# Latent attention's gate product dealt out between the rounds of attention, and the last additions in another order

## The chip, the cores and the metric

The kernel runs on one core of a Trainium2 chip. What is measured is the device time of one execution in microseconds. The kernel before takes 1385.15 us (median of three, 1384.3 to 1385.21).

## The reference

Two transformer blocks over 512 tokens of 1024 features, all in float32. The first puts 16 meta tokens ahead of the sequence and mixes in three ways: a short convolution, latent attention with a gate, and retention.

```python
(cx, cb, cc, cz, cq, ckv, krope, mz, rq, rk, rv, rz) = jnp.split(u @ w_in[l], IN_OFFSETS, axis=-1)
y_conv = short_conv_mixer(cx, cb, cc, cz, ...)      # b * conv3(c * x) * silu(z)
y_mla = mla_mixer(cq, ckv, krope, mz, ...)          # 8 heads, chunked mask; softmax(q k) v * silu(mz)
y_ret = retention_mixer(rq, rk, rv, rz, ...)        # 4 heads, rotary q and k; rms_norm(o) * silu(rz)
h = h + jnp.concatenate([y_conv, y_mla, y_ret], axis=-1) @ w_out[l]
```

The second block has gated linear attention, sparse attention, attention to a memory of 256 rows, and a mixture of 16 experts of which each token takes two:

```python
hid = jax.nn.silu(hf @ w_gate[e]) * (hf @ w_up[e])
out = sum over the two chosen experts of share * (hid @ w_down[e])
x + out
```

## The kernel before

All five engines walk through one list of steps that `make_order` writes, and each issues its own instructions of a step. Nothing else sets the order: if a step stands later in the list, it stands later in the queue of every engine that has to do with it. Engines wait for each other by counters; a wait holds up all that is queued behind it on its engine.

A dense product in full precision is made of three matmuls, high part by high part, high by low and low by high (`product`, L1036 to L1038). Weights come in units of two chunks of 128 rows by 512 columns; SyncE loads them, ScalarE writes the high part (L1801), GpSimd the low part (L917), four units ahead at most. A "part" is what one unit adds to one of four PSUM banks: six matmuls of 512 columns. A product by 1024 features has four units and so 16 parts (and, for retention, four short ones for the meta rows, in bank 4).

The stretch in question: the latent part, the queries and keys of latent attention (`w_uq`, `w_ukv`), the two convolution products `conv_a` and `conv_b`, the convolution itself on VectorE (`conv`, L3046 to L3058), the rotation and scaling of queries (VectorE, L3139 to L3143) and keys (GpSimd, L928, L930) in `mla_norm`, the gate product `mla_z`, and then `mla_order`: 16 rounds, m = 0 to 15, four for each pair of heads, in which the query tile is m % 4. A round does two heads, j = 2m and 2m + 1:

- `mla_scores`: a TensorE product (L1202), VectorE's maximum (L3153), ScalarE's exp (L2315)
- `mla_prob`: VectorE divides by the sum (L3163, L3166)
- `mla_turn`: TensorE transposes the probabilities, first the 16 meta columns into bank 4 (L1209), then the others into bank 6 (L1212); VectorE copies the first (L3172), ScalarE the others (L2323)
- `mla_values`: TensorE, for the round before (L1227, L1230); behind the fourth tile VectorE multiplies by the gate (L3179)

The scores of a round with the last tile are 528 wide and take part of bank 4 too, so that they wait until VectorE has copied the meta columns of the head before. Every new pair begins with `mla_transposes` of its two heads (L1181 to L1187), copied by ScalarE (L2301, L2307).

Between these stand the steps that `take` deals out, two parts or one step of retention at a time: the products `ret_qk` and `ret_vz`, retention's transposes, scores, values and turns for each pair of its heads, and one unit of the output product `w_out0`. Then `mix_mla` writes high and low parts of the gated output (L2368, L2519).

`ret_qk` is rotated by VectorE in `rope_turn`: four products of the PSUM bank with cosine or sine into the temporaries t0 to t3 (L2534 to L2537), and from these a difference and a sum (L2539, L2540). There is one set of temporaries.

At the very end stands `last_rows`: experts 14 and 15 are visited last, and their share is added through one-hot products instead of memory. `down` writes a visit's output into banks 5 and 6, ScalarE and VectorE make high and low parts (L2068, L3014), TensorE spreads them to the tokens (L1640, L1641) in eight banks by `ROW_BANKS`. The other experts' rows come back by gathers from GpSimd's queue (L994), two for each token tile; `add(t)` scales and adds them (L3026, L3028), and L3038 adds the one-hot rows; SyncE stores each tile.

## Time and profile before

| | us |
|---|---|
| median of three runs | 1385.15 |
| the profiled execution | 1386.81 |
| its span | 1385.0 |
| TensorE busy | 1294.7 |
| VectorE busy | 644.0 |
| ScalarE busy | 633.8 |
| GpSimd busy | 408.7 |

The rounds of latent attention lie between 139 and 304 us of the span, the last down product begins at 1361.7 us. Times in the rows are from the start of the span. In the timelines a row is one instruction or several like it, and what stands in brackets is how long its engine had been idle and what ended that. The granted clock (PEclk) is 1.00 for TensorE at 2.4 GHz and 0.50 at 1.2 GHz; a mean between says how the stretch is divided. A matmul's end is modelled, so starts are the safer numbers.

### The profile page before, as it was taken

The numbers are of one execution on the slowest core, as the hardware profiler recorded it, in microseconds if no ns is written. First come the engines' busy times: TensorE is split into PE (matmuls) and PEld (weight loads), VectorE is DVE, ScalarE is ACT, GpSimd is POOL, SyncE is SP. The second block draws the span as 40 slices with busy tenths as digits, with TensorE's granted clock in tenths as the row PEclk, the third lists the DMA queues.
The fourth block names the chain that finished last, engine by engine and source line by source line (L and its number), as shares of the span: only waits on it lengthen the run. The fifth ranks groups of instructions, "written<-read, shape, count | busy, mean of one in ns | idle before, by whom it ended". The sixth has DMA issues, their size and how long they took to land.

```text
span 1385.0 us, 16953 instructions
## 1 busy us (share of the span) xinstructions
PE 1294.7 (93%) x6321; PEld 1000.8 (72%) x6321; DVE 644.0 (46%) x1423; ACT 633.8 (46%) x1105; POOL 408.7 (30%) x202
## 2 busy tenths in 40 slices
PE   5999889879989999999998998999999999899996
PEld 4798666557768777775887786888787777676764
DVE  3255354535230125236898444314334133777775
ACT  5443434343552457445334545333433323577771
POOL 4265221014655341232533222444105431100002
PEclk9999999979999999999999999999999999999998
DMA  5243423013445221221332111342107430799935
GB/s 166 66 127 107 136 94 122 18 60 117 152 132 167 77 73 50 61 77 46 112 94 69 47 55 60 114 152 79 36 1 257 180 140 36 296 420 412 421 147 199
DMA packets 76317, 179.13 MB, mean 129 GB/s; under 512 B 11184, under 2 KB 22758, under 8 KB 69574
## 3 DMA queue, kind: packets, MB, share of 16 engines
q1 hardware_dynamic: 68528, 164.96, 34.8%
q0 software_dynamic: 2592, 8.40, 1.6%
q10 hardware_dynamic: 5110, 4.62, 1.2%
q8 instruction: 53, 0.87, 0.3%
q14 instruction: 34, 0.28, 0.1%
HBM read 152.79 MB, written 25.17 MB: 128 GB/s over the span
## 4 chain that ended last, share of the span: by engine, by line
PE 81%; DVE 10%; ACT 4%; issue 3%; DMA 1%; POOL 0%; SPq 0%; DVEq 0%; ACTq 0%; POOLq 0%
PE ps L1036 20%; PE ps L1037 20%; PE ps L1038 20%; PE ps L1574 4%; PE ps L1202 1%; PE ps L1442 1%; PE ps L1425 1%; PE ps L1558 1%; DVE mix_lo L2519 1%; DVE work L2740 1%; PE ps L1398 1%; PE ps L1230 1%; DVE best L2738 1%; PE ps L1470 1%; PE ps L1432 1%
## 5 line engine op out<-in xcount | busy, mean ns | idle before, releaser
L917 POOL TENSOR_TENSOR w_lo<-raw,w_hi 128x1024 fp32r<-128x1024 f32 (+1 forms) x158 | 378.2, 2408 | 754.8 <-ACT w_hi L1801 745.9
L1801 ACT ACTIVATE w_hi<-raw 128x1024 fp32r<-128x1024 f32 (+1 forms) x158 | 159.8, 1032 | 170.4 <-PE ps L1038 162.1
L1036 PE MATMUL ps<-w_hi,act_hi 128*128 128x512 f32 (+1 forms) x560 | 232.3, 415 | 3.1 <-DVE gate L2601 0.9
L1037 PE MATMUL ps<-w_lo,act_hi 128*128 128x512 f32 (+1 forms) x560 | 219.1, 391 | 0.0
L1038 PE MATMUL ps<-w_hi,act_lo 128*128 128x512 f32 (+1 forms) x560 | 218.3, 390 | 0.0
L1036 PE MATMUL ps<-w_hi,mix_hi 128*128 128x512 f32 x320 | 132.8, 415 | 7.7 <-DVE mix_lo L2519 6.4
L1036 PEld LDWEIGHTS ps<-w_hi,act_hi 128*128 128x128 f32 (+1 forms) x560 | 104.3, 186 | 40.3 <-issue 11.9
L1037 PE MATMUL ps<-w_lo,mix_hi 128*128 128x512 f32 x320 | 127.0, 397 | 0.0
L1038 PE MATMUL ps<-w_hi,mix_lo 128*128 128x512 f32 x320 | 126.8, 396 | 0.0
L1038 PEld LDWEIGHTS ps<-w_hi,act_lo 128*128 128x128 f32 (+1 forms) x560 | 104.0, 186 | 24.9
L1037 PEld LDWEIGHTS ps<-w_lo,act_hi 128*128 128x128 f32 (+1 forms) x560 | 104.2, 186 | 23.7 <-issue 1.2
L1036 PE MATMUL ps<-act_hi,w_hi 128*128 128x512 f32 (+4 forms) x280 | 100.9, 362 | 2.0 <-DVE act_lo L2514 1.0
L1037 PE MATMUL ps<-act_lo,w_hi 128*128 128x512 f32 (+4 forms) x280 | 100.7, 362 | 0.0
L1038 PE MATMUL ps<-act_hi,w_lo 128*128 128x512 f32 (+4 forms) x280 | 100.1, 360 | 0.0
L2973 DVE SCALAR_TENSOR_TENSOR gu_lo<-gu,g,e_hi 128x512 fp32r<-128x512 f32 x120 | 82.3, 746 | 24.6 <-ACT e_hi L2034 24.6
L2034 ACT ACTIVATE e_hi<-gu,g 128x512 fp32r<-128x512 f32 x120 | 79.5, 718 | 11.6 <-PE ps L1038 11.3
L1036 PEld LDWEIGHTS ps<-w_hi,mix_hi 128*128 128x128 f32 x320 | 61.9, 193 | 23.2 <-DVE mix_lo L2519 7.2
L1037 PEld LDWEIGHTS ps<-w_lo,mix_hi 128*128 128x128 f32 x320 | 61.9, 193 | 13.5 <-issue 1.0
L1038 PEld LDWEIGHTS ps<-w_hi,mix_lo 128*128 128x128 f32 x320 | 61.5, 192 | 13.3
L1574 PE MATMUL ps<-dn,hidT 128*128 128x512 f32 x128 | 59.3, 608 | 2.3 <-DVE yl_lo L3014 2.3
L1036 PEld LDWEIGHTS ps<-act_hi,w_hi 128*128 128x128 f32 (+2 forms) x280 | 51.5, 184 | 12.4 <-DVE act_lo L2514 1.1
L1038 PEld LDWEIGHTS ps<-act_hi,w_lo 128*128 128x128 f32 (+2 forms) x280 | 51.5, 185 | 9.6 <-issue 0.5
(472 smaller groups left out, 2114.3 us busy)
## 6 DMA issues: line engine op xcount, KB each, us to landing
raw<-in_w_in SPq DMA_DIRECT2D x92, 512.0 KB, 3.6
gu<-in_w_gate SPq DMA_DIRECT2D x16, 1024.0 KB, 7.8
gu<-in_w_up SPq DMA_DIRECT2D x16, 1024.0 KB, 10.0
dn<-in_w_down SPq DMA_DIRECT2D x16, 1024.0 KB, 10.1
x_rows<-zeros SPq DMA_DIRECT2D x16, 512.0 KB, 5.0
raw<-in_w_out SPq DMA_DIRECT2D x16, 512.0 KB, 4.1
raw<-in_w_mem_kv SPq DMA_DIRECT2D x16, 512.0 KB, 3.8
xe<-x_rows SPq DMA_DIRECT2D x15, 512.0 KB, 10.8
```

Of the source, the lines that this page charges most:

```text
L917: pool.tensor_tensor(lo[:, 0:a], raw[:, g % RAW_SLOTS, 0:a], hi[:, 0:a].bitcast(F32), ALU.subtract).then_inc(*POOL.done(("w_lo", g)))
L1036: pe.matmul(dst, l_hi, r_hi, start=start, stop=False, skip_group_check=skip)
L1037: pe.matmul(dst, l_hi, r_lo, start=False, stop=False, skip_group_check=skip)
L1038: return pe.matmul(dst, l_lo, r_hi, start=False, stop=stop, skip_group_check=skip)
L1202: mm = pe.matmul(psf[:, at + a:at + b], q, kT[0:QKH, i, a:b], start=True, stop=True)
L1230: mm = pe.matmul(dst[i], v_sb[:, b, cols[i]], probT[:, i, P * b:P * b + P], start=False, stop=(b == t))
L1398: pe.matmul(ps[:, bank, 0:n], iqT[rows, h // 2, P * t:P * t + P], ikT[rows, 0:n], start=True, stop=True).then_inc(*PE.done(("rel", t, h)))
L1425: pe.matmul(ps[:, 4 + j % 2, 0:n], dqT[:, h, P * t:P * t + P], dkT[:, h // DSA_G, 0:n], start=True, stop=True).then_inc(*PE.done(("d_S", j)))
L1574: mm = pe.matmul(ps[:, 5 + n, :], hidT[:, i, P * c:P * c + P], dn[s][:, c, 512 * n:512 * n + 512], start=(c == 0), stop=(c == 1))
L1801: nc.scalar.activation(split_slot(g)[0][:, 0:a], raw[:, g % RAW_SLOTS, 0:a], ACTF.Copy).then_inc(*ACT.done(("w_hi", g)))
L2034: nc.scalar.activation(e_hi[:, k, :, :], gu[s][:, :, k, :], ACTF.Copy, scale=g8[:, k:k + 1]).then_inc(*ACT.done(("e_hi", e, k)))
L2973: dve.scalar_tensor_tensor(gu_lo[s][:, :, k, :], gu[s][:, :, k, :], g8[:, k:k + 1], e_hi[:, k, :, :].bitcast(F32), ALU.mult, ALU.subtract) ...
```

## The change

It has five pieces:

1. The gate product `mla_z` no longer stands ahead of the rounds. Its 16 parts head the list that `take` deals from, now in single parts; a round gets two for each head, a round with the last tile one, round 5 four more. Three `w_out0` parts are left for behind round 15.
2. ScalarE copies the gate's product out of PSUM (`z_raw`) and does silu for all four banks in one instruction over 2048 columns in round 4 (`mla_gate`), with the table loads around it.
3. `mla_norm` for the second half of queries and keys stands within `conv_b`; the convolution of the second 128 features and the copying of the high parts (`conv_high`) come later.
4. Retention's difference and sum go to GpSimd for the four full tiles (`ret_turned`); VectorE waits for GpSimd before it writes the temporaries again.
5. At the end tile 1 is added ahead of the last visit's low parts, that visit's down product uses banks 0 and 1, tiles 0 and 1 are finished ahead of tile 3, tile 3's first scaling goes to ScalarE and its first addition to GpSimd, and its store is cut in two.

```diff
-ROW_BANKS = (0, 1, 2, 3, 4, 7, 5, 6)
+ROW_BANKS = (5, 6, 2, 3, 4, 7, 0, 1)
+DOWN_BANKS = [5] * (N_EXP - 1) + [0]
...
-    fill = item("ret_qk", "ret_vz")
-    fill = [fill[i:i + 2] for i in range(0, len(fill), 2)]
+    fill = [[x] for x in item("mla_z", "ret_qk", "ret_vz")]
...
+    def take(n):
+        taken = []
+        while fill and n > 0:
+            n -= 1 if fill[0][0][0] == "part" else 2
+            taken += fill.pop(0)
+        return taken
+
+    order = take(3) + [("mla_transposes", 0), ("conv", 1)] + take(1) + [("mla_transposes", 1)] + take(1)
...
-                order += [("mla_transposes", 2 * m // NT)] + take() + [("mla_transposes", 2 * m // NT + 1)]
+                order += [("mla_transposes", 2 * m // NT)] + take(2) + [("mla_transposes", 2 * m // NT + 1)] + take(1)
...
+        n = 0 if m == turns else 1 if m % NT == NT - 1 else 2
+        order += take(n + 4 * (m == NT + 1))
...
+        if m == 0:
+            order += [("conv_high", 0), ("conv_high", 1)]
+        if m == NT:
+            order += [("mla_gate",)]
...
-    order += [("mla_sums",)] + item("conv_a") + [("mla_norm", 0), ("mla_norm", 1)] + item("conv_b") + [("conv",)]
-    order += [("mla_norm", t) for t in range(2, NT + 1)] + item("mla_z")
+    cb = item("conv_b")
+    order += [("mla_sums",)] + item("conv_a") + [("mla_norm", 0), ("mla_norm", 1)] + cb[0:2] + [("mla_norm", 2)] + cb[2:4]
+    order += [("mla_norm", 3)] + cb[4:6] + [("mla_norm", NT)] + cb[6:] + [("conv", 0)]
...
-    order += [("gather",), ("add", 0), ("down", N_EXP - 1), ("add", 1), ("add", 2), ("add", 3), ("last_rows",), ("overflow",)]
+    order += [("gather",), ("add", 0), ("add", 1), ("down", N_EXP - 1), ("add", 2), ("x_last", 0), ("x_last", 1), ("add", 3)]
+    order += [("last_rows",), ("x_last", 2), ("x_last", 3), ("overflow",)]
...
+            def ret_turned(t):
...
+                pool.wait_ge(*DVE.after("rope_r", t, 3))
+                pool.tensor_tensor(out[:, :, 0:32], tmp[0], tmp[1], ALU.subtract).then_inc(*POOL.done(("rope_r", t, 4)))
+                pool.tensor_tensor(out[:, :, 32:64], tmp[2], tmp[3], ALU.add).then_inc(*POOL.done(("rope_r", t, 5)))
...
+                elif step == "add" and a[0] == NT - 1:
+                    pool.wait_ge(*ACT.after("y_share", a[0]))
+                    pool.tensor_tensor(yg[:, 2 * a[0], :], yg[:, 2 * a[0], :], x1[:, a[0], :], ALU.add).then_inc(*POOL.done(("x", "first", a[0])))
...
+            def mla_gate():
+                act.wait_ge(*ACT.after("z_raw", NT - 1))
+                tables(SILU)
+                nc.scalar.activation(z_mla[:, :, :], z_mla[:, :, :], ACTF.Silu).then_inc(*ACT.done(*[("z_mla", p) for p in range(4)]))
+                tables(LN_EXP)
...
+                    if b:
+                        dve.wait_ge(*POOL.after("rope_r", b - 1, 5))
```

Where the change moves instructions, three places stand here as they are in an engine's queue. The same instruction has a line number 28 to 52 higher in the kernel after.

The first is VectorE's queue where retention's tiles 1 and 2 are rotated, before (t0 to t3 are the temporaries, sm the softmax's sums, prob its probabilities):

```order
L2534 TENSOR_TENSOR t0_85<-ps,rope_82 128x256
L2535 TENSOR_TENSOR t1_86<-ps,rope_82 128x256
L2536 TENSOR_TENSOR t2_87<-ps,rope_82 128x256
L2537 TENSOR_TENSOR t3_88<-ps,rope_82 128x256
L2539 TENSOR_TENSOR rqk_79<-t0_85,t1_86 128x8x32
L2540 TENSOR_TENSOR rqk_79<-t2_87,t3_88 128x8x32
L2534 TENSOR_TENSOR t0_85<-ps,rope_82 128x256
L2535 TENSOR_TENSOR t1_86<-ps,rope_82 128x256
L2536 TENSOR_TENSOR t2_87<-ps,rope_82 128x256
L2537 TENSOR_TENSOR t3_88<-ps,rope_82 128x256
L2539 TENSOR_TENSOR rqk_79<-t0_85,t1_86 128x8x32
L2540 TENSOR_TENSOR rqk_79<-t2_87,t3_88 128x8x32
```

and after:

```order
L2581 TENSOR_TENSOR t0_85<-ps,rope_82 128x256
L2582 TENSOR_TENSOR t1_86<-ps,rope_82 128x256
L2583 TENSOR_TENSOR t2_87<-ps,rope_82 128x256
L2584 TENSOR_TENSOR t3_88<-ps,rope_82 128x256
L2581 TENSOR_TENSOR t0_85<-ps,rope_82 128x256
L2582 TENSOR_TENSOR t1_86<-ps,rope_82 128x256
L2583 TENSOR_TENSOR t2_87<-ps,rope_82 128x256
L2584 TENSOR_TENSOR t3_88<-ps,rope_82 128x256
L3215 RECIPROCAL sm_64<-sm_64 128x1
L3218 TENSOR_SCALAR prob_101<-prob_101,sm_64 128x272
L3224 COPY probT_m_100<-ps 16x128
```

The two sums of a tile are gone from the queue, and two tiles stand directly one behind the other, with GpSimd's sums between them.

The second is TensorE's queue at the fourth pair of heads, from the transposes of its second head on, before (q_sb and k_sb are queries and keys, rqT and rkT retention's, sd and sd_m its scores times the decay):

```order
L1181 MATMUL ps<-ident,q_sb 96x128 x4
L1185 MATMUL ps<-ident,k_sb 96x16
L1187 MATMUL ps<-ident,k_sb 96x128 x4
L1202 MATMUL ps<-kT,qT 128x144
L1267 MATMUL ps<-rqT,rkT 128x256 x2
L1267 MATMUL ps<-rqT,rkT 128x128 x2
L1273 MATMUL ps<-rqT,rkT 16x512 x2
L1209 MATMUL ps<-ident,prob 16x128
L1212 MATMUL ps<-ident,prob 128x128 x4
L1202 MATMUL ps<-kT,qT 128x144
L1286 MATMUL ps<-sd_m,rv 64x512 x2
```

and after, from the same transposes on:

```order
L1209 MATMUL ps<-ident,q_sb 96x128 x4
L1213 MATMUL ps<-ident,k_sb 96x16
L1215 MATMUL ps<-ident,k_sb 96x128 x4
L1295 MATMUL ps<-rqT,rkT 128x256 x2
L1295 MATMUL ps<-rqT,rkT 128x128 x2
L1301 MATMUL ps<-rqT,rkT 16x512 x2
L1230 MATMUL ps<-kT,qT 128x144
L1314 MATMUL ps<-sd_m,rv 64x512 x2
L1319 MATMUL ps<-sd,rv 64x512 x2
L1319 MATMUL ps<-sd,rv 64x384 x2
```

Retention's two last score steps (the rows with rqT; of them only those of 256 columns and less stand in this piece) now come between the transposes and the first scores, and its values follow when only these scores stand between.

The third is VectorE's queue at the end, before (yl are the last two visits' rows, yg the gathered ones):

```order
L3014 SCALAR_TENSOR_TENSOR yl_lo<-ps,slot_share,yl_hi 128x512 x2
L3026 SCALAR_TENSOR_TENSOR yg<-yg,share,x_56 128x1024
L3028 SCALAR_TENSOR_TENSOR yg<-yg,share 128x1024
L3014 SCALAR_TENSOR_TENSOR yl_lo<-ps,slot_share,yl_hi 128x512 x2
L3026 SCALAR_TENSOR_TENSOR yg<-yg,share,x_56 128x1024
L3028 SCALAR_TENSOR_TENSOR yg<-yg,share 128x1024
L3026 SCALAR_TENSOR_TENSOR yg<-yg,share,x_56 128x1024
L3028 SCALAR_TENSOR_TENSOR yg<-yg,share 128x1024
L3026 SCALAR_TENSOR_TENSOR yg<-yg,share,x_56 128x1024
L3028 SCALAR_TENSOR_TENSOR yg<-yg,share 128x1024
L3038 TENSOR_TENSOR yg<-ps,yg 128x512 x8
```

and after:

```order
L3062 SCALAR_TENSOR_TENSOR yl_lo<-ps,slot_share,yl_hi 128x512 x2
L3075 SCALAR_TENSOR_TENSOR yg<-yg,share,x_56 128x1024
L3079 SCALAR_TENSOR_TENSOR yg<-yg,share 128x1024
L3075 SCALAR_TENSOR_TENSOR yg<-yg,share,x_56 128x1024
L3079 SCALAR_TENSOR_TENSOR yg<-yg,share 128x1024
L3062 SCALAR_TENSOR_TENSOR yl_lo<-ps,slot_share,yl_hi 128x512 x2
L3075 SCALAR_TENSOR_TENSOR yg<-yg,share,x_56 128x1024
L3079 SCALAR_TENSOR_TENSOR yg<-yg,share 128x1024
L3088 TENSOR_TENSOR yg<-ps,yg 128x512 x4
L3079 SCALAR_TENSOR_TENSOR yg<-yg,share 128x1024
L3088 TENSOR_TENSOR yg<-ps,yg 128x512 x4
```

Tile 1's additions stand ahead of the second low parts, four of the eight last sums ahead of tile 3's second addition, and tile 3's first addition has left the queue.

## Rows read from the trace of the kernel before

**Rows 1.** The page: busy time, and the chain that ended last, by engine.

```profile
PE 1294.7 (93%) x6321; PEld 1000.8 (72%) x6321; DVE 644.0 (46%) x1423; ACT 633.8 (46%) x1105; POOL 408.7 (30%) x202
...
PE 81%; DVE 10%; ACT 4%; issue 3%; DMA 1%; POOL 0%; SPq 0%; DVEq 0%; ACTq 0%; POOLq 0%
```

**Rows 2.** TensorE timeline: start us, us, instruction [idle, releaser]; new pairs.

```profile
141.23 0.64 PE L1181 MATMUL ps<-ident,q_sb 128*96 128x128 f32 x4 [1.43 <-ACT qT L2301]
...
143.55 0.48 PE L1202 MATMUL ps<-kT,qT 96*128 96x144 f32 x2 [0.88 <-ACT kT L2307]
...
264.80 0.48 PE L1202 MATMUL ps<-kT,qT 96*128 96x144 f32 x2 [0.88 <-ACT kT L2307]
```

**Rows 3.** TensorE timeline, waits behind the rotary products.

```profile
160.56 0.27 PE L1209 MATMUL ps<-ident,prob 128*16 128x128 f32 x1 [0.60 <-DVE sm L3163]
...
188.64 0.27 PE L1209 MATMUL ps<-ident,prob 128*16 128x128 f32 x1 [2.02 <-DVE rqk L2633]
```

**Rows 4.** TensorE timeline, among retention's steps.

```profile
238.81 1.45 PE L1258 MATMUL ps<-rqT,rkT 64*128 64x512 f32 x6 [0.36 <-ACT probT L2323]
...
254.71 1.16 PE L1202 MATMUL ps<-kT,qT 96*128 96x128 f32 x4 [1.43 <-DVE probT_m L3172]
```

**Rows 5.** TensorE timeline, round 15 and the gap behind it.

```profile
286.28 1.16 PE L1202 MATMUL ps<-kT,qT 96*128 96x128 f32 x4 [1.06 <-DVE probT_m L3172]
...
290.37 2.12 PE L1202 MATMUL ps<-kT,qT 96*128 96x128 f32 x4 [1.01 <-DVE probT_m L3172]
...
303.87 0.77 PE L1036 MATMUL ps<-w_hi,mix_hi 128*128 128x512 f32 x1 [2.83 <-DVE mix_lo L2519]
```

**Rows 6.** Stretches: busy us of PE, PEld, DVE, ACT, POOL; then PEclk, DMA.

```profile
117.00:138.00 21.00, 20.62 (x89) 16.36 (x88) 15.65 (x14) 9.13 (x11) 10.25 (x4) 1.00 0.41 118
186.00:194.00 8.00, 5.98 (x27) 4.61 (x26) 5.28 (x21) 2.44 (x6) 1.34 (x1) 0.79 0.00 0
286.00:310.00 24.00, 17.62 (x76) 11.96 (x77) 7.52 (x21) 11.33 (x16) 2.37 (x1) 0.57 0.07 19
```

**Rows 7.** VectorE timeline, the end.

```profile
1367.90 1.41 DVE L3014 SCALAR_TENSOR_TENSOR yl_lo<-ps,slot_share,yl_hi 128x512 fp32r<-128x512 f32 x2 [3.94 <-ACT yl_hi L2068]
1369.23 1.27 DVE L3026 SCALAR_TENSOR_TENSOR yg<-yg,share,x 128x1024 f32<-128x1024 f32 x1
...
1376.78 4.87 DVE L3038 TENSOR_TENSOR yg<-ps,yg 128x512 f32<-128x512 f32 x8
```

**Rows 8.** TensorE timeline, round 3: the second head's scores.

```profile
170.46 1.16 PE L1202 MATMUL ps<-kT,qT 96*128 96x128 f32 x4
```

**Rows 9.** VectorE timeline: round 3's meta copy; retention's tiles 1 and 2.

```profile
170.12 0.28 DVE L3172 COPY probT_m<-ps 16x128 f32<-16x128 f32 x1 [0.23 <-PE ps L1209]
...
180.66 0.42 DVE L2534 TENSOR_TENSOR t<-ps,rope 128x256 f32<-128x256 f32 x1 [2.28 <-PE ps L1038]
...
182.11 0.42 DVE L2539 TENSOR_TENSOR rqk<-t,t 128x256 f32<-128x256 f32 x1
...
182.98 0.43 DVE L2534 TENSOR_TENSOR t<-ps,rope 128x256 f32<-128x256 f32 x1
```

**Rows 10.** ScalarE timeline: the gate by 512 columns, and its table load.

```profile
134.50 1.28 ACT L1809 ACT_TABLE_LOAD   x1 [6.50 <-PE ps L1038]
135.79 1.09 ACT L1937 ACTIVATE z_mla<-ps 128x512 f32<-128x512 f32 x2
```

**Rows 11.** GpSimd timeline: half a tile of keys, scaled.

```profile
110.44 0.62 POOL L930 TENSOR_TENSOR k_sb<-kr,ss 128x256 f32<-128x256 f32 x1
```

**Rows 12.** TensorE and ScalarE timelines, the last down product and its hidden rows.

```profile
1361.71 5.37 PE L1574 MATMUL ps<-dn,hidT 128*128 128x512 f32 x8 [2.27 <-DVE yl_lo L3014]
...
1360.41 0.38 ACT L2056 ACTIVATE hidT<-ps 128x256 f32<-128x256 f32 x1
```

**Rows 13.** VectorE and GpSimd timelines, a product beside a weight split.

```profile
312.77 2.59 DVE L3218 TENSOR_TENSOR y_ret<-y_ret,z_ret 128x256 f32<-128x256 f32 x1
...
312.68 2.40 POOL L917 TENSOR_TENSOR w_lo<-raw,w_hi 128x1024 fp32r<-128x1024 f32 x1 [5.28 <-ACT w_hi L1801]
```

More of the change, by code:

```diff
@@ L212, in mla_order @@
     tail = item("w_out0")
-    fill += [tail[0:2], tail[2:4]]
-    def take():
-        return fill.pop(0) if fill else []
-    order = [("mla_transposes", 0), ("mla_transposes", 1)]
+    fill += [[x] for x in tail[0:4]]
+    def take(n):
[5 more added lines that the diff above has]
+    order = take(3) + [("mla_transposes", 0), ("conv", 1)] + take(1) + [("mla_transposes", 1)] + take(1)
     for m in range(turns + 1):
@@ L232, in mla_order @@
             order += [("mla_scores", 2 * m + 1)]
-        order += take()
+        order += take(n)
         if m < turns:
             order += [("mla_prob", 2 * m + 1)]
+        if m == 0:
+            order += [("conv_high", 0), ("conv_high", 1)]
+        if m == NT:
+            order += [("mla_gate",)]
         if m:
             order += [("mla_values", m - 1)]
-    while fill:
-        order += take()
+    order += take(2 * len(fill))
     order += [("mix_mla",)] + tail[4:8] + [("ret_norm",)] + tail[8:12] + [("mix_ret",)] + tail[12:]
@@ L895, in _ @@
                 sp.dma_start(expert_rows(y_rows, expert_of(e - 1)), ye[:, (e - 1) % 2, :]).then_inc(ye_out[(e - 1) % 2], 16)
-            for t in range(NT):
+            for t in range(NT - 1):
                 sp.wait_ge(*DVE.after("x", LAST, t))
                 sp.dma_start(out[0, P * t:P * (t + 1), :], yg[:, 2 * t, :]).then_inc(stored, 16)
-            sp.wait_ge(stored, 16 * NT)
+            for n, key in enumerate((("x", "left", NT - 1), ("x", LAST, NT - 1))):
+                sp.wait_ge(*DVE.after(*key))
+                cols = slice(512 * n, 512 * n + 512)
+                sp.dma_start(out[0, P * (NT - 1):P * NT, cols], yg[:, 2 * NT - 2, cols]).then_inc(stored, 16)
+            sp.wait_ge(stored, 16 * (NT + 1))
         @block.gpsimd
@@ L1007, in _ @@
                     split_low(min(len(units), first_unit[a[0]] + 3))
-                elif step == "part" and split_upto(*a):
-                    split_low(split_upto(*a))
+                elif step == "part":
+                    if split_upto(*a):
+                        split_low(split_upto(*a))
+                    if a[0] == "ret_qk" and a[1] == n_units("ret_qk") - 1 and a[2] != "meta":
+                        ret_turned(a[2])
                 elif step == "first_split":
@@ L2421, in _ @@
                     norm_square(*a)
-                elif step == "conv":
-                    for b in range(2):
-                        act.wait_ge(*DVE.after("cy", b))
-                        nc.scalar.activation(mix_hi[:, b, :], cy[:, b, :], ACTF.Copy).then_inc(*ACT.done(("conv_hi", b)))
+                elif step == "conv_high":
+                    b = a[0]
+                    act.wait_ge(*DVE.after("cy", b))
+                    nc.scalar.activation(mix_hi[:, b, :], cy[:, b, :], ACTF.Copy).then_inc(*ACT.done(("conv_hi", b)))
                 elif step == "latent_sums":
@@ L2524, in rope_turn @@
             def rope_turn(key, x, out, rows, heads, half, t, cos, sin):
-                n = heads * half
+                if key == ("rope_r", NT):
+                    dve.wait_ge(*POOL.after("rope_r", NT - 1, 5))
                 if turned:
@@ L2529, in rope_turn, with rope_products @@
                 turned.append(key)
+                tmp = rope_products(key, x, rows, heads, half, t, cos, sin)
+                dve.wait_ge(*DVE.after(*key, 3))
+                dve.tensor_tensor(out[:, :, 0:half], tmp[0], tmp[1], ALU.subtract).then_inc(*DVE.done((*key, 4)))
+                dve.tensor_tensor(out[:, :, half:2 * half], tmp[2], tmp[3], ALU.add).then_inc(*DVE.done((*key, 5)))
+            def rope_products(key, x, rows, heads, half, t, cos, sin):
+                n = heads * half
                 tmp = [b[0:rows, 0:n].rearrange("p (h n) -> p h n", h=heads) for b in (t0, t1, t2, t3)]
@@ L2537, in rope_turn @@
                 dve.tensor_tensor(tmp[3], b, c, ALU.mult).then_inc(*DVE.done((*key, 3)))
[L2538 to L2540 removed]
+                return tmp
             def evict(name, b):
@@ L3028, in add @@
                 dve.scalar_tensor_tensor(y, yg[:, 2 * t + 1, :], share[:, 1, t:t + 1], y, ALU.mult,
                                          ALU.add).then_inc(*DVE.done(("x", "second", t)))
-            def last_rows():
-                for t in range(NT):
-                    dve.wait_ge(*DVE.after("x", "second", t))
-                    for n in range(2):
-                        y = yg[:, 2 * t, 512 * n:512 * n + 512]
-                        dve.wait_ge(*PE.after("rows", t, n))
-                        dve.tensor_tensor(y, ps[:, ROW_BANKS[2 * t + n], :], y,
-                                          ALU.add).then_inc(*DVE.done(*([("x", LAST, t)] if n else [("x", "left", t)])))
```

103 lines of the change are left out of this document (58 added, 45 removed).

## The prediction

> **What bounds the kernel now.** First the page: TensorE is busy 93% of the span, and the chain that ended last runs through it for 81% [rows 1]. So what counts is where TensorE waits, where its clock falls, and the end, where VectorE takes over. Then the timeline of TensorE over the rounds of latent attention (139 to 304 us; in rounds 3, 7, 11 and 15 the query tile is the last and longest). It waits 24 times for more than 0.3 us there, 22.1 us in sum, in five kinds:
> - at each new pair of heads for ScalarE's copy of the turned queries or keys: 1.43 once and 0.88 four times, the first and last of them in [rows 2], 4.95 us in all
> - for VectorE, late with the rotary products of retention: 0.60 twice, 0.81, 2.02, together 4.03 us [rows 3] (first and last of four)
> - among retention's steps five waits from 0.36 to 1.43, together 3.14 us [rows 4]
> - in round 15 and behind it, where nothing is left to deal out, six waits from 0.47 to 2.83, together 7.16 us [rows 5]
> - at the pairs 0.69 three times and 0.79 once, together 2.86 us, for copies that the new order doesn't cover either; they stay.
>
> Next the clock in the table by stretches: TensorE was granted 0.79 over 186 to 194, around the wait of 2.02, and 0.57 over 286 to 310, in the stretch of the last waits, against 1.00 in the dense product before [rows 6]. Last the end: after a wait of 3.94 us VectorE works from 1367.90 to 1381.65 without a break [rows 7].
>
> **The gate product dealt out.** Nothing is removed: 16 parts of six matmuls, at 21 us / 89 x 6 = 1.42 us a part [rows 6], make 22.7 us before and after. Five of them now stand around the first transposes, the rest fill rounds 0 to 2, and all that stood in the rounds moves back by so much, so that there is something to deal out until round 15, and three products of the output weight are left for the gap behind it. Kind by kind:
>
> (a) A part or a retention step now stands between each pair's transposes and its first scores. 1.42 covers 0.88, and the 1.43 went to a table load of ScalarE that is no longer there. Gain 4.95.
>
> (b) Rounds with the last tile now get one part for each head instead of two. In round 3 TensorE came to the second head's scores at 170.46 without a wait [rows 8]. But they need the bank that VectorE's copy of the meta columns frees, and this ran at 170.12 for 0.28; its engine had finished the first head's softmax, which stands ahead of it, only 0.23 before [rows 9]. With a part less TensorE is there 1.4 us sooner and VectorE is not. Less the 0.2 of slack, rounds 3 and 7 lose 1.2 each: 2.4. What was dealt there works elsewhere, so this is a true loss, and the reason why I don't take most of the 22 us for gain.
>
> (c) The gap behind round 15. The wait of 2.83 goes to the last gating and to its high and low part; three products, 4.3 us, now stand there. Round 15 gets one retention step of 0.6 us and one part. Its two scores stay at the distance that the softmax sets, 4.09 us before (286.28 to 290.37 [rows 5]); I leave 2.2 there, 0.7 ahead of the last transposes and 0.9 ahead of the last values. 7.16 becomes 3.8, gain 3.4.
>
> (d) Retention's steps meet rounds 11 to 15 instead of 8 to 13. The same as before, except that its values now follow its meta scores with only one head's scores between, while VectorE has some 1.2 us of decay product to do. 3.14 becomes 3.9, loss 0.75.
>
> **The gate's silu** is now one ScalarE instruction over 2048 columns between two table loads of 1.28 [rows 10]: with 1.09 for two of 512, some 2 us, and 4.5 together. Behind it in ScalarE's queue stand a copy of round 4's probabilities and the next exp, and VectorE waits for it as well. TensorE has six parts there (7.8 us): cost 0. Without that cover it would be 4.5 us; a gain is excluded, since TensorE never waited for the four that go.
>
> **Queries turned ahead of the convolution.** VectorE stood idle through most of the convolution's product; the second half of the queries goes there, and the keys on GpSimd with it, while the convolution itself now ends some 3 us ahead of the first softmax. Cost 0, between -0.5 and +1.5 (one weight split of GpSimd in the way).
>
> **Rotary sums on GpSimd.** A tile cost VectorE products of 1.45 us (180.66 to 182.11) and two sums, 2.32 from tile to tile [rows 9]. The sums go. But the four temporaries are single, so VectorE may start the next tile only when GpSimd has read them: two sums, by the nearest GpSimd row 0.62 each [rows 11], and the hand-overs, 1.4 us. For tiles that come close upon each other, as 1 and 2 do, the period becomes 2.85 instead of 2.32, and in front of the first GpSimd may be at a weight split of 2.4 us. By this the meta part, the next transposes and round 7's scores behind them wait about 1.8, 1.8 and 0.6: 4.2 against 4.03. I take 0, between -2 and +3.
>
> So the waits fall by 4.95 + 3.4 - 2.4 - 0.75 = 5.2 us.
>
> **The clock.** A mean of 0.57 over 24 us says 20.6 us at the lower level, 1.2 GHz, and the rest at 2.4. TensorE was busy 17.6 us of it [rows 6], some 15 of these slow: at full clock up to 7.5 less, or about 6 where waits set the pace. Ahead of the fall stood the waits of rounds 14 and 15. These are better filled now but still have waits of 1 to 2 us; I count half, 3 us, with 0 and 6 as ends. The fall around the rotary wait (0.79 of 8 us: 3.4 us slow, 1.7 lost) stays.
>
> Attention together: 5.2 + 3.0 = 8.2 us less.
>
> **The end.** Now the additions of tile 1 (2.5 us a pair: 1.27 of [rows 7] and its like) go into the wait of 3.94. The last down product takes banks 0 and 1 and waits no longer for VectorE until 1361.71, but only for its hidden rows on ScalarE, 1360.41 + 0.38 [rows 12]: it starts at 1360.9. It took 5.37 while the clock was down; its like at full clock is 3.45. So the low parts could begin at 1365.1 to 1367.1, but VectorE has tile 1 until 1366.5. From there it has 13.75 - 2.5 for tile 1 - 1.27 for the first addition of tile 3, which goes to ScalarE and GpSimd, = 10.0 us: the end comes at 1376.5 to 1377.1 instead of 1381.65. Tile 3's scaling waits for its gather (some 1369.6), then 1.1 on ScalarE and 2.4 on GpSimd, as for a weight split [rows 13]: ready at 1373.1, when VectorE asks for it at 1372.9. Gain 4.9, and 0.1 for the smaller last store: 5.0, between 2.5 and 5.6.
>
> Here a row speaks against the change. A VectorE product of two SBUF operands took 2.59 us where it began at 312.77, 0.09 behind a GpSimd subtraction of 2.40 [rows 13]; of the same size and kind, the one at 182.11 took 0.42 [rows 9]. The Trainium skill ("SBUF — State Buffer", section "Who interferes with whom") says that a VectorE instruction with two SBUF inputs and a GpSimd instruction that reads SBUF exclude each other for the whole instruction, whichever starts first. By that rule, the trace agrees, GpSimd's addition could hold up VectorE's on tile 2, while the last sums, with one operand in PSUM, run on.
>
> **Sum.** The profiled execution took 1386.8 us, its span 1385.0 and 1.8 around it: 1386.8 - 8.2 - 5.0 = 1373.6. It lies 1.7 above the median of 1385.15, so 1371.9, or 1372.
>
> **Rivals.**
> 1. The fill works better: VectorE's copies come sooner and the clock stays up through round 15; waits of 12 us are left instead of 17. For it: with two parts as fill TensorE never waits in rounds 5 to 7. Against it: the copy at 170.12 [rows 9]. Attention gives 14, time 1366. Chance 0.20.
> 2. The waits only move: GpSimd's sums and the single parts cost 5 more and the clock falls as before, so that the end alone remains: 1380. For it: VectorE's tight queue in rounds 5 and 6. Against it: kind (a) needs no luck. Chance 0.15.
> 3. The exclusion at the end: GpSimd's addition starts between the two of tile 2, and VectorE stands 2.4 us: 1374.5. It decides whether GpSimd begins before VectorE's second instruction of tile 2; the gather's time speaks for later. Chance 0.12.
> 4. Slower: the clock falls where only small products are left, rounds 11 to 15, and stays at 1.2 GHz through them. Like work over 235 to 275 kept TensorE busy some 35 us; slow it would take 20 more, of which the waits hide 5, and the 3 of the clock term go as well: 1372 + 15 + 3 = 1390. It turns to slower from about 25 us at half clock. Against it: the same steps ran at full clock before. Chance 0.04.
>
> **Numbers.** The forecast keeps 0.49. A measurement can tell about 0.2%, 2.8 us, from no change: faster is below 1382.4. The forecast, rivals 1 and 3 and two thirds of rival 2 lie there: faster 0.91; same 0.05 from the rest of rival 2; slower 0.04. The range goes from 1364, beyond rival 1's centre, to 1380, the centre of rival 2, with under 0.2 outside.
>
> **What would show it.** Right: second heads' scores in rounds 3 and 7 with a new wait of 1.0 to 1.4 us; none before a pair's first scores; none of 2.8 behind the last values; VectorE waiting for GpSimd between retention's tiles 1 and 2; VectorE's last sum 4 to 5 us nearer to the last up product. Wrong: waits over the rounds below 13 or above 21 us; half clock over more than 12 us behind round 13, or none at all; a VectorE addition of over 3 us at the end; ScalarE's silu on TensorE's path.

## The result, and the profile after

| | median, us | runs | ratio to before, 95% interval |
|---|---|---|---|
| before | 1385.15 | 1383.8 to 1386.55 | |
| changed | 1374.66 | 1372.86 to 1378.42 | 0.9927 [0.9912, 0.9942] |

The change makes the kernel 10.5 us faster by the medians (8.0 to 12.2 by the interval). The forecast was 1372 in a range from 1364 to 1380: the direction and the range hold, the gain is 2.7 us smaller than the forecast. A second series on another chip gave 1373.77 against 1384.05, ratio 0.9916 [0.9901, 0.9932].

The profiled execution took 1372.86 with a span of 1371.0, so it is the fastest of the five; that of before was 1.7 above its median. The difference of the two spans, 1385.0 and 1371.0, is 14.0 us and therefore more than the change is worth. The two rows of the page, as in [rows 1], say little: TensorE is as busy as before, in a shorter span.

```profile
PE 1292.2 (94%) x6321; PEld 1000.1 (73%) x6321; DVE 636.5 (46%) x1414; ACT 636.3 (46%) x1107; POOL 416.4 (30%) x211
...
PE 71%; DVE 8%; ACT 3%; issue 3%; POOL 1%; DMA 0%; DVEq 0%; ACTq 0%; POOLq 0%
```

**TensorE's waits in the rounds.** From 139 us to the end of the last values the timeline now has 17 waits over 0.3 us, 15.3 us in sum, for 24 and 22.1. A pair's first scores, which waited 0.88 [rows 2], now run without one. The rows below are, in order of time, the second head's scores of round 3, which had no wait [rows 8], the first scores of a new pair, the two waits behind retention's rotary products, and the second head's scores of round 7 (start, duration, instruction, idle time before it and who ended it):

```profile
152.36 1.16 PE L1230 MATMUL ps<-kT,qT 96*128 96x128 f32 x4 [1.10 <-DVE probT_m L3224]
...
163.43 0.41 PE L1230 MATMUL ps<-kT,qT 96*128 96x144 f32 x2
...
188.28 0.29 PE L1064 MATMUL ps<-w_hi,act_hi 128*16 128x256 f32 x1 [2.31 <-DVE probT_m L3224]
...
190.75 0.37 PE L1237 MATMUL ps<-ident,prob 128*16 128x128 f32 x1 [1.60 <-DVE rqk L2681]
...
202.93 1.16 PE L1230 MATMUL ps<-kT,qT 96*128 96x128 f32 x4 [1.11 <-DVE probT_m L3224]
```

In round 15 and the gap behind it, which had 7.16 [rows 5], four are left, 3.16 us. The last row is the output product that had waited 2.83:

```profile
278.37 0.27 PE L1237 MATMUL ps<-ident,prob 128*16 128x128 f32 x1 [0.46 <-DVE sm L3205]
...
280.39 1.16 PE L1230 MATMUL ps<-kT,qT 96*128 96x128 f32 x4 [1.43 <-DVE probT_m L3224]
...
285.44 0.66 PE L1240 MATMUL ps<-ident,prob 128*128 128x128 f32 x4 [0.39 <-ACT probT L2354]
...
286.98 0.43 PE L1255 MATMUL ps<-probT_m,v_sb 16*64 16x128 f32 x4 [0.88 <-ACT probT L2354]
...
288.37 0.50 PE L1064 MATMUL ps<-w_hi,mix_hi 128*128 128x512 f32 x1
```

**The clock.** The table by stretches, as in [rows 6] (busy time of the five engines, then the granted clock): the stretch from 286 to 310, which had 0.57, has 0.98. The fall around the rotary waits is longer than before, and there is a short one behind 308.

```profile
189.00:197.00 8.00, 6.40 (x19) 4.61 (x17) 4.96 (x19) 2.96 (x6) 1.80 (x3) 0.57 0.01 2
286.00:310.00 24.00, 20.36 (x103) 16.15 (x103) 12.10 (x21) 12.03 (x16) 7.84 (x4) 0.98 0.52 167
308.00:313.00 5.00, 5.00 (x16) 3.93 (x16) 1.38 (x2) 0.00 (x0) 2.22 (x1) 0.66 0.79 258
```

This execution had luck with its clock. In the profile of e8 below, which is the same kernel on another chip, the same waits stand in round 15 (0.46, 1.43, 0.39 and 0.88), but the clock falls among them, where it is 1.00 here, and the fall behind 308 is twice as long:

```profile
280.00:290.00 10.00, 7.97 (x54) 5.26 (x56) 2.82 (x9) 3.69 (x7) 2.35 (x1) 0.83 0.13 40
308.00:316.00 8.00, 6.32 (x16) 5.00 (x17) 2.79 (x4) 1.66 (x3) 2.37 (x1) 0.57 0.62 197
```

Of the seven profiles with this order of steps in round 15 and these waits, five have the fall at 280 us (e2, e3, e8, e10, e11) and two have not (this one and e7). So that the clock stays up through round 15 is not something the change brings every time.

**The end.** Tile 1's additions stand in what was a wait of 3.94 [rows 7], the last down product starts on its hidden rows alone, and VectorE waits 0.31 for GpSimd's addition. These are TensorE's, VectorE's and GpSimd's rows:

```profile
1350.89 3.67 PE L1602 MATMUL ps<-dn,hidT 128*128 128x512 f32 x8 [1.51 <-ACT hidT L2081]
```

```profile
1355.49 1.28 DVE L3079 SCALAR_TENSOR_TENSOR yg<-yg,share 128x1024 f32<-128x1024 f32 x1
1356.69 1.40 DVE L3062 SCALAR_TENSOR_TENSOR yl_lo<-ps,slot_share,yl_hi 128x512 fp32r<-128x512 f32 x2
...
1359.32 1.28 DVE L3079 SCALAR_TENSOR_TENSOR yg<-yg,share 128x1024 f32<-128x1024 f32 x1
1360.53 2.48 DVE L3088 TENSOR_TENSOR yg<-ps,yg 128x512 f32<-128x512 f32 x4
1363.31 1.28 DVE L3079 SCALAR_TENSOR_TENSOR yg<-yg,share 128x1024 f32<-128x1024 f32 x1 [0.31 <-POOL yg L1048]
1364.52 2.48 DVE L3088 TENSOR_TENSOR yg<-ps,yg 128x512 f32<-128x512 f32 x4
```

```profile
1360.82 2.39 POOL L1048 TENSOR_TENSOR yg<-yg,x 128x1024 f32<-128x1024 f32 x1 [6.08 <-ACT yg L2103]
```

**Where the 14.0 us between the traces lie.** Three places that both kernels pass: the first transposes of the memory rows behind attention, at 336.82 and 325.85 (11.0 ahead); the end of the last up product, at 1355.8 and 1345.7 (10.1 ahead, since the clock fell once more in between); the span's end (14.0). So attention is 10.1 and the end 3.9 of it.

### The profile page after: what moved, and what is told of

Read it like the earlier page. It is cut to its first block, busy times and chain, and to the rows that moved or that the text cites. A ratio compares the mean times of both kernels' runs of the same rounds, so it can differ in the third digit from the quotient of the medians.

```text
span 1371.0 us, 16957 instructions
## 1 busy us (share of the span) xinstructions
PE 1292.2 (94%) x6321; PEld 1000.1 (73%) x6321; DVE 636.5 (46%) x1414; ACT 636.3 (46%) x1107; POOL 416.4 (30%) x211
## 4 chain that ended last, share of the span: by engine, by line
PE 71%; DVE 8%; ACT 3%; issue 3%; POOL 1%; DMA 0%; DVEq 0%; ACTq 0%; POOLq 0%
PE ps L1064 17%; PE ps L1065 17%; PE ps L1066 17%; PE ps L1602 4%; PE ps L1470 1%; PE ps L1453 1%; PE ps L1586 1%; PE ps L1230 1%; DVE mix_lo L2557 1%; DVE work L2788 1%; PE ps L1426 1%; DVE best L2786 1%; PE ps L1573 1%; PE ps L1498 1%; PE ps L1460 1%
## 5 line engine op out<-in xcount | busy, mean ns | idle before, releaser
L2059 ACT ACTIVATE e_hi<-gu,g 128x512 fp32r<-128x512 f32 x120 | 79.5, 718 | 11.9 <-PE ps L1066 11.6
## 6 DMA issues: line engine op xcount, KB each, us to landing
dn<-in_w_down SPq DMA_DIRECT2D x16, 1024.0 KB, 10.2
```

Source lines behind the costliest of these rows:

```text
L2059: nc.scalar.activation(e_hi[:, k, :, :], gu[s][:, :, k, :], ACTF.Copy, scale=g8[:, k:k + 1]).then_inc(*ACT.done(("e_hi", e, k)))
```

## The experiments

The first four, and then the next four, and then the last three ran on one chip each, with runs of before between them (medians 1386.22, 1384.05, 1384.36).

**e1, the end alone, and e2, attention alone.**

```
  # e1: before.py, with
+ order += [("gather",), ("add", 0), ("add", 1), ("down", N_EXP - 1), ("add", 2), ("x_last", 0), ("x_last", 1), ("add", 3)] ...
+ ROW_BANKS = (5, 6, 2, 3, 4, 7, 0, 1); DOWN_BANKS = [5] * (N_EXP - 1) + [0]
  # and tile 3's first addition on ScalarE and GpSimd, last store in halves
  # e2: after.py, with all of that as in before.py
```

> The kernel before with the end of the new one alone: order of the additions, banks 0 and 1 for the last down product, tile 3's first addition on ScalarE and GpSimd, last store in two halves. My theory: the two parts of the change are independent and the end is worth what the two traces show from the last up product's end to the last instruction, 29.6 - 25.7 = 3.9 us, so some 1381.2 against 1385.15. Rival: the end depends on the state of the clock (TensorE's last down product took 5.37 us in the trace of before and 3.67 in the new one), and with the clock up in both it is worth under 2.5: above 1382.6. Second rival, the forecast's first number: 5.0, some 1380.

> The new kernel with the end of before: the changes in attention alone. My theory: 10.5 of the medians less 3.9 for the end, 6.6 us less than before: some 1378.6. Rival 'waits only move': under 3 us less, above 1382. Rival 'the clock term is the larger one': 10 or 11 us less as in the profiled execution, 1374 to 1375, which would leave nothing for the end.

e1: 1381.58, ratio 0.9970 [0.9959, 0.9982], 4.2 us. e2: 1375.71, ratio 0.9932 [0.9915, 0.9949], 9.4 us. The end is worth what the traces say (3.9), though its interval goes from 2.5 to 5.7 us, so that the rival under 2.5 is only just outside and the forecast's 5.0 is inside. Attention gives more than the 6.6 I had left for it, which lies outside e2's interval (7.1 to 11.8), and nearly all of the 10.1 that the traces show. The two ratios add up to 13.6 us, the whole gave 10.1 and 11.6; the intervals reach over that, and the runs don't say more.

**e3, the rotary sums back on VectorE.**

```
-                         ret_turned(a[2])       # GpSimd's two sums, per tile
...
+                    rope_turn(("rope_r", b), ...  # VectorE's four products and two sums, as before
```

> The new kernel with retention's rotary sums back on VectorE. My theory (the forecast's term of 0, between -2 and +3): a tile has a period of 2.32 on VectorE alone and 3.02 with GpSimd (182.63 to 185.65 in the new trace), so TensorE's two waits of 2.31 and 1.60 become shorter by 1 to 2 us in sum and the time falls by as much: 1372.7 to 1373.7. Rival: taking the sums off VectorE is worth something (its last softmax steps come sooner), waits grow by 1 to 2: 1376. A difference below 1 us either way is the forecast's 0.

1374.23, ratio 0.9923 [0.9910, 0.9936]: no difference to the changed kernel. TensorE's two waits are 2.19 and 2.42 there, 4.61 in sum, against 3.91 with GpSimd: the shorter waits that I expected did not come, and the rival's sign is right with less than its size. Why they nearly cancel is in VectorE's rows. Changed kernel, then GpSimd's first sum there, then e3:

```profile
181.05 0.87 DVE L3218 TENSOR_SCALAR prob<-prob,sm 128x272 f32<-128x272 f32 x1
...
182.63 0.41 DVE L2581 TENSOR_TENSOR t<-ps,rope 128x256 f32<-128x256 f32 x1
...
185.65 0.42 DVE L2581 TENSOR_TENSOR t<-ps,rope 128x256 f32<-128x256 f32 x1 [1.61 <-POOL rqk L953]
```

```profile
181.03 0.74 POOL L952 TENSOR_TENSOR rqk<-t,t 128x256 f32<-128x256 f32 x1 [1.05 <-DVE sm L3215]
```

```profile
180.75 0.36 DVE L3211 TENSOR_SCALAR prob<-prob,sm 128x272 f32<-128x272 f32 x1
...
181.82 0.41 DVE L2577 TENSOR_TENSOR t<-ps,rope 128x256 f32<-128x256 f32 x1
...
184.13 0.42 DVE L2577 TENSOR_TENSOR t<-ps,rope 128x256 f32<-128x256 f32 x1
```

With GpSimd a tile that follows closely comes 3.02 us behind the one before it (182.63 to 185.65), with VectorE alone 2.31. And the scaling of 272 probabilities takes 0.87 beside GpSimd's sums and 0.36 without them. Together they cost most of what the sums gave; 0.7 us of wait are left. The Trainium skill ("SBUF — State Buffer", section "Who interferes with whom") says that a VectorE scaling by a scalar can enter a mode that also takes the port pair shared with GpSimd, and that whichever of the two issues first then holds it for its whole instruction while the other stands. The trace agrees: GpSimd's sum began at 181.03 and lasted 0.74, VectorE's scaling began 0.02 later and took 0.87 where it takes 0.36 for the same size without GpSimd.

**e4, two parts in the rounds of the last tile.**

```
- n = 0 if m == turns else 1 if m % NT == NT - 1 else 2
+ n = 0 if m == turns else 2
```

> The new kernel with two parts for each head in rounds 3, 7, 11 and 15 too, as the kernel before dealt them. My theory: the waits of 1.10 and 1.11 us for the meta copy in rounds 3 and 7 go (this is the loss of 2.4 that the forecast took), but the steps run out sooner by four parts or steps, so that round 15 and the gap behind it have waits again, 2 to 4 us more, and perhaps the clock falls there: 0 to 4 us slower, some 1376. Rival: the loss in rounds 3 and 7 is the larger, and the kernel gets 2 us faster: 1372.5.

1382.75, ratio 0.9972 [0.9961, 0.9982]: by the ratios 6 to 8 us slower than the changed kernel (0.9927 and 0.9916), where I gave 4 as the most. The waits of 1.10 and 1.11 are gone, as said, and that of 2.83 behind the last values is back. In sum TensorE waits 2.8 us longer than in e2, which has the changed kernel's attention (21.3 against 18.5 from 100 to 345 us). The rest is the clock. TensorE's waits ahead of its falls, then the stretches of e4:

```profile
187.16 0.39 PE L1064 MATMUL ps<-w_hi,act_hi 128*16 128x256 f32 x1 [4.00 <-DVE probT_m L3224]
...
244.32 2.13 PE L1230 MATMUL ps<-kT,qT 96*128 96x128 f32 x4 [3.09 <-DVE probT_m L3224]
```

```profile
185.00:196.00 11.00, 8.85 (x31) 5.94 (x32) 7.56 (x28) 2.85 (x6) 3.60 (x5) 0.53 0.05 18
243.00:261.00 18.00, 15.20 (x63) 6.56 (x64) 6.74 (x18) 2.93 (x6) 0.00 (x0) 0.62 0.11 33
294.00:309.00 15.00, 10.97 (x59) 8.10 (x58) 5.02 (x12) 9.84 (x13) 2.37 (x1) 0.66 0.08 22
```

(1 - 0.53) x 2 x 11 and so on give 34 us at half clock, against 10 in the changed kernel's trace and 17 in e8's. The memory transposes come at 336.21, where the changed kernel has 325.85. One number in the order of the steps is worth 6 to 8 us; the waits account for 2.8 of it, and for the rest the trace has nothing but the clock.

**e5, zeros in the waits of before.** 55 matmuls that add zero to an open sum, in round 15 and the gap, in front of instructions that wait there (shortened; all six places are in round 15 and behind it).

```
+ for _ in range(n):    # n = 8, 7, 8, 3, 7 and 22
+     pe.matmul(ps[:, bank, 0:256], left[:, 0, 0:P], zeros[:, :].bitcast(F32R), start=False, stop=False)
```

> The kernel before, with TensorE's waits of round 15 and of the gap behind it filled by 55 small matmuls that add zero to an open sum (256 columns each, 0.12 us from one to the next: 6.6 us for waits of 7.2). No wait of another engine is touched. Theory 'clock': what the change gained in attention beyond its shorter waits is the clock; with TensorE kept busy it stays at its higher level over 286 to 310 us, where it was 0.57, and the kernel gets 5 to 7 us faster although nothing was taken away: about 1379.5. Rival 'waits': the time follows the waits alone, the zeros stand in them and the time stays within 1 us of 1385.5, or gets up to 2 worse where a filler is longer than its wait.

1384.20, ratio 0.9996 [0.9985, 1.0008]: nothing gained. The prediction of theory 'clock' failed, though its first half came true. The clock stays up, and TensorE is through with the output products 6.1 us sooner (the last begins at 310.57, for 316.72 in before). But VectorE's work from the gating to retention's norm, which the transposes behind them wait for, is only 4.1 sooner (its first instruction at 297.01 for 301.09, its last at 313.24 for 317.32): four waits stand there where there had been one of 0.36. And behind those and the 1.83 that follows the clock falls after all. Stretches, TensorE and VectorE of e5:

```profile
286.00:310.00 24.00, 22.54 (x150) 18.32 (x149) 10.66 (x25) 12.52 (x19) 3.79 (x2) 1.00 0.20 67
314.00:322.00 8.00, 6.17 (x19) 4.75 (x18) 2.36 (x4) 2.21 (x3) 2.36 (x1) 0.57 0.58 196
```

```profile
311.43 0.30 PE L1686 MATMUL ps<-ident,y_ret 128*128 128x128 f32 x1 [0.47 <-DVE y_ret L3226]
312.13 0.33 PE L1686 MATMUL ps<-ident,y_ret 128*128 128x128 f32 x1 [0.40 <-DVE y_ret L3226]
312.93 0.33 PE L1686 MATMUL ps<-ident,y_ret 128*128 128x128 f32 x1 [0.46 <-DVE y_ret L3226]
313.72 0.77 PE L1686 MATMUL ps<-ident,y_ret 128*128 128x128 f32 x5 [0.47 <-DVE y_ret L3226]
```

```profile
297.01 0.69 DVE L3187 TENSOR_TENSOR z_mla<-ps,z_mla 128x512 f32<-128x512 f32 x1 [2.52 <-PE ps L1235]
...
308.71 2.57 DVE L3226 TENSOR_TENSOR y_ret<-y_ret,z_ret 128x256 f32<-128x256 f32 x1
...
313.24 0.42 DVE L3226 TENSOR_TENSOR y_ret<-y_ret,z_ret 128x256 f32<-128x256 f32 x1
```

Of 6.1 us, 4.1 are left behind the transposes (316.32 for 320.40), and 1.7 at the memory rows (335.15 for 336.82). The trace shows the gain given back, first to VectorE and then to the clock of a later place. Of VectorE's chain 2.57 are the product beside a weight split of GpSimd that takes 0.42 otherwise, as in before [rows 13]: there this cost is on the path. The changed kernel still pays it (2.58 at 300.18, beside a weight split that began at 300.09).

**e6, zeros in the changed kernel's waits at 188 us.** 16 of them ahead of the last product of retention's tile 3, 8 ahead of the last of its meta columns.

```
+ if name == "ret_qk" and last and b == NT - 1:
...
+     idle(b, 16, act_hi)
...
+ if name == "ret_qk" and u == last_u and j == len(chunks) - 1:
+     idle_meta(8)
```

> The new kernel with 24 such matmuls of zeros in the waits of 2.31 and 1.60 us at 188 to 191 us (16 ahead of the last product of retention's tile 3, 8 ahead of the last product of its meta columns). Theory 'clock': the clock, at half from 189.5 to 196.7 us in the trace, stays up, and TensorE's work of 191 to 196.7 takes half the time: 2.5 to 3.5 us faster than the new kernel beside it. Rival 'waits': no change within 1 us.

1370.16, ratio 0.9892 [0.9875, 0.9909]; the changed kernel beside it (e8) 1373.77, ratio 0.9916 [0.9901, 0.9932]. So 3.3 us by the ratios and 3.6 by the medians, for 24 instructions that compute nothing. The two intervals overlap a little, but each of e6's six runs (1366.55 to 1371.21) is below each of e8's six (1371.64 to 1375.57). The stretch of 189 to 197, 0.57 in the changed kernel, is at 1.00:

```profile
189.00:197.00 8.00, 7.02 (x44) 4.77 (x41) 4.73 (x19) 2.91 (x7) 2.22 (x3) 1.00 0.00 0
...
253.00:258.00 5.00, 5.00 (x25) 2.42 (x24) 0.74 (x3) 0.86 (x3) 0.00 (x0) 0.66 0.31 118
```

```profile
190.34 0.27 PE L1252 MATMUL ps<-ident,prob 128*16 128x128 f32 x1 [0.70 <-DVE rqk L2699]
...
196.06 1.16 PE L1245 MATMUL ps<-kT,qT 96*128 96x128 f32 x4 [0.28 <-DVE probT_m L3242]
```

VectorE's work is the same, and the transposes at 190.34 start where they did (190.75; e6's execution is 0.4 ahead from 152 us on). From them to the scores at 196.06 it is 5.7 us, where it had been 8.1 (to 198.84): 2.4 us gained by the clock alone. The rest of the 3.3 is not explained by this place. In e6's profile the falls at 280 and behind 308 are missing too, though the waits there are the same as in the changed kernel (0.46, 1.43, 0.39, 0.89 and 0.47, 0.47, 1.83), and only a short one at 254 to 258 stands from 100 us to the memory rows. One trace doesn't show whether the fillers are the reason. e6 is, with e9, the fastest of the versions that were run.

**e7, one last store, and e8, the changed kernel again.**

```
- for n, key in enumerate((("x", "left", NT - 1), ("x", LAST, NT - 1))): ...   # two halves
+ for t in range(NT): ...                                                      # four whole tiles
```

> The new kernel with its last store whole again (512 KB behind the second sum of tile 3). In the traces the last instruction lies 4.00 us behind VectorE's last sum with two halves and 3.35 with one. Theory: the second half waits for a fixed time of its own and for the 1 MB ahead of it, and the cut costs 0.3 to 0.7 us. Rival (the forecast): the cut gains 0.1, so this kernel is 0.1 slower. Third: the tail is bound by the rate of the DMA engines, which show 360 to 450 GB/s there, and nothing changes.

> The new kernel unchanged, beside the three others, so that they are compared on one chip: expected 1374 to 1375, with executions from 1373 to 1378 that differ in the granted clock.

e7: 1372.28, ratio 0.9912 [0.9896, 0.9929], which can't be told from e8. The last instruction lies 3.9 us behind the last sum in both. The intervals are too wide for my 0.3 to 0.7 or the forecast's 0.1, but the tails of the two traces are alike to 0.02 us: the cut is worth nothing that shows. What makes the tail longer than the 3.35 of before, and the 3.3 of e2, is the order: in those the four stores follow each other without a break, in e7 and e8 there is a pause behind the second. A pause alone isn't the reason, though: in e11 it is longer, and the tail is 3.2 us. This stays open.

**e9, more zeros.** e6, with 6 ahead of the last values and 14 behind retention's norm.

```
+ order += [("idle", 6)] * (m == turns) + [("mla_values", m - 1)]
+ [("mix_ret",), ("idle", 14)] + tail[12:]
```

> The kernel of e6 (24 matmuls of zeros at 188 to 191 us) with 6 more ahead of the last values of latent attention and 14 ahead of the output products behind retention's norm (0.12 us each, into waits of 0.88 and 1.83 us). Theory 'clock': the stretch at half clock behind the wait of 1.83, 308 to 313 us in the trace of the new kernel, goes as well: 1.0 to 1.7 us less than e6, some 1369, 15.5 to 16.5 us less than before. Rival: as in e5 the clock falls a little later instead, and the time is that of e6, 1370. Second rival: the fillers run over their waits and it is 0.5 to 1 slower than e6.

1370.73, ratio 0.9899 [0.9878, 0.9920], not to be told from e6. Of e9's profile alone one could say that the fall behind 308 is gone; but e6's profile hasn't got it either, without these fillers, and e9's has one at 239 to 247 that e6's hasn't. So neither is shown to come from the fillers.

**e10, no silu.** The gate's silu and its two table loads are left out; the gate's product is used as it is.

```
- tables(SILU)
- nc.scalar.activation(z_mla[:, :, :], z_mla[:, :, :], ACTF.Silu) ...
- tables(LN_EXP)
+ nc.scalar.activation(z_mla[:, 0, 0:1], z_mla[:, 0, 0:1], ACTF.Copy) ...   # one column, for the signal
```

> The new kernel without the silu of latent attention's gate (the gate's product is used as it is) and without the two table loads around it: ScalarE has 4.5 us less to do at 168.7 to 173.2. Theory (the forecast's cost of 0): six parts of TensorE lie beside it, the time stays within 1 us of the new kernel's, 0.9916 to 0.9927 of before. Rival: the gate is on TensorE's path and its 4.5 us, less what is hidden, show: 2 us or more faster. Second rival: the gate delays the rotary products on VectorE and with them the waits of 2.31 and 1.60, which become shorter: 1 to 2 us faster.

1374.03, ratio 0.9934 [0.9913, 0.9955]. TensorE's waits are those of e2 (18.46 and 18.48 us from 140 us on), the two at 188 us too, with 2.31 and 1.60. So the gate costs nothing where it stands, as far as 3 us of interval and the equal waits can tell.

**e11, tile 3's first addition back on VectorE.**

```
- else: dve.wait_ge(*POOL.after("x", "first", t))
+ dve.scalar_tensor_tensor(y, y, share[:, 0, t:t + 1], x1[:, t, :], ALU.mult, ALU.add) ...   # for tile 3 too
```

> The new kernel with tile 3's first addition back on VectorE. Theory: VectorE is busy without a break to the end, so its 1.28 us count, less the 0.31 it waits for GpSimd in the trace: 1.0 us slower, ratio to before higher by 0.0007. Rival (two engines on SBUF exclude each other): GpSimd's addition costs VectorE as much as it saves, no difference.

1373.98, ratio 0.9923 [0.9904, 0.9942]: 1 us above e8's ratio, within both intervals. VectorE's part is in the traces: from the first addition to the last sum it takes 16.57 us there (1352.02 to 1368.59) and 15.68 in the changed kernel, 0.9 longer. But behind the last sum e11's trace ends after 3.2 us and the changed kernel's after 4.0, so that from the first addition to the end of the span the two are 19.8 and 19.7. What GpSimd's addition is worth at the end of the kernel is not shown.

## Why the prediction was right, and where it was off

**Waits.** By kind, forecast and measured, from the changed kernel's timeline:

| | before | forecast | after |
|---|---|---|---|
| (a) a pair's first transposes and scores | 4.95 | 0 | 0 |
| rotary products | 4.03 | 4.0 | 5.3 |
| retention's steps | 3.14 | 3.9 | 1.7 |
| (c) round 15 and behind it | 7.16 | 3.8 | 3.2 |
| (b) second heads, rounds 3 and 7 | 0 | 2.4 | 2.2 |
| those that stay | 2.86 | 2.9 | 2.9 |
| sum | 22.1 | 16.9 | 15.3 |

The two that argued from one slack (0.23 us ahead of the meta copy [rows 9]) and from one cover (1.42 for 0.88) came out within 0.2. The loss at retention's steps was not there. The rotary term was too low by 1.3: the period of 2.85 is 3.02, GpSimd's sums take 0.73 and 0.79 and not 0.62, and VectorE's scaling beside them 0.87. It lies within its range of -2 to +3. But two of the four waits were misread. The 0.60 at 160.56 and the 0.81 at 172.43 in before end ahead of VectorE's first rotary product (174.90), behind the softmax; two like them, 0.81 and 0.59, stand in the changed kernel at 240.48 and 241.95, at retention's values, which are not rotated. The rotary products alone went from 2.6 us of wait to 3.9.

**The clock.** The term was 3.0, between 0 and 6. In the two profiled executions TensorE is 11.0 us ahead at the memory rows; the waits give 6.8 of it, 0.4 a wait of before at 127 us that is gone, and two waits of 0.47 and 0.46 for one of 0.36 take 0.6 back. So 4.4 are left, and I put them down to the clock. But executions differ: six profiles with the changed attention and end or store as they may be (after, e2, e7, e8, e10, e11) reach that place at 325.2 to 328.9, 326.65 in the mean, two with the old one (before, e1) at 336.82 and 335.81. That is 9.7, and 3.1 are left for the clock in the same way. The granted clock bears this out: from 100 to 346 us the six stand at 1.2 GHz for 10.2 to 17.1 us, 13.7 in the mean, and before and e1 for 23.9 and 20.5; half of the difference, 4.3, is the most that it can give. The forecast's half was the right size in the mean, and the size changes from one execution to the next. But its reason was incomplete. e5 shows that keeping TensorE busy through round 15 gains nothing by itself: VectorE's norm came only 4.1 us sooner, and the clock fell behind it. In the changed kernel VectorE begins this work 12.6 us sooner (288.49 for 301.09), since real work moved. e6 shows the reverse: the fall at 188 us, which I had left as it was at 1.7 us, got longer (0.79 over 186 to 194 [rows 6], now 0.57 over 189 to 197), and with the fillers that take it away the kernel is 3.3 us faster.

**The gate, the queries.** Cost 0 for the gate: e10 agrees. (The six parts that were to cover it are 8.5 us by the forecast's own 1.42 each, and not 7.8; nothing hangs on it.) TensorE has no wait over 0.3 us in its first rounds before 152 us, so the queries cost none there; they were not tried alone.

**The end.** This is the term that was off. The forecast was 5.0, the traces have 3.9, e1 4.2 [2.5, 5.7]. Step by step it held. The start of the last down product was put at 1360.9, which is 1350.8 in the changed kernel's time; it is 1350.89. GpSimd's sum was put at 1373.1 and VectorE's call for it at 1372.9, that is 1363.0 and 1362.8; they are 1363.21 and 1363.00. VectorE's end of 1377.1 is 1367.0; it is 1367.00. VectorE's last sum is 4.6 us nearer to the last up product (21.3 for 25.9). What failed is the last step, 0.1 for the smaller store: from the last sum to the end it takes 4.00 us for 3.35, so 0.7 were lost, and not by the cut of the store (e7). The other 0.3 are because VectorE's end came at the later edge of my range.

**The rivals.** Rival 1 (the fill works better, 1366) is a third true: 15.3 us of waits, between my 16.9 and its 12. Rival 2, that the waits only move, did not come: they fell by 6.8, and e2 alone gives 9.4 us. Rival 3, the exclusion at the end, missed by 0.2 us: GpSimd's addition began at 1360.82, when VectorE had just ended its second on tile 2 at 1360.60. VectorE's sums with one operand in PSUM run beside it at 0.62 each (2.48 for four), as they did in 4.87 for eight [rows 7]. Rival 4, the clock low through the last rounds, did not come with the change, but e4 comes near it, with falls at 185, 243 and 294 us: one part dealt otherwise, and more than half the gain of the whole change is lost.

**The sum.** 13.2 was forecast, 10.1 [8.0, 12.2] and 11.6 [9.4, 13.7] measured. 1.1 of the difference is the end. Terms from the traces, 9.7 for attention by the place at the memory rows or 9.2 by the first expert (1196.0 for 1205.3 in the same means), and 3.9 for the end, come to 13.1 to 13.6, as e1 and e2 do, and the two series of the whole kernel lie lower. This stays open; executions of one kernel differ by up to 5.6 us here (1372.86 at a granted clock of 0.985, 1378.42 at 0.980), and that is more than what is missing.

## What to carry to other kernels

Look for waits kind by kind, and ask of each what stands ahead of it in its releaser's queue: a copy behind another head's softmax doesn't come sooner because TensorE does. Read the clock beside the waits. Where it fell here, the work behind the waits lost time that is of the order of the waits themselves (2.4 us behind 3.9 at 189 us). A filler of useless matmuls in a wait that can't be shortened can give some of that back, if no other engine sets the pace right behind it: e6 gained 3.3 us and e5 nothing. And take several profiles of one kernel before a fall of the clock is put down to a wait. Try the number of steps dealt out per round by measuring: its effect through the clock can't be had from the waits alone.
